# Decode attention products in four column groups: one step of a hybrid decoder trunk on one Trainium2 core

## The reference

```python
# differential attention, decode: 4 heads, two maps of 32 each, 1024 cached keys in pages of 128
past_k = cache_diff_k[page_table, l]; k_all = concat([past_k, ck]); v_all = concat([past_v, cv])
s = einsum('bqhmd,bkhmd->bhmqk', q, k_all) * 32 ** -0.5 + bias
p = softmax(s); o_c = einsum('bhqk,bkhe->bqhe', p[:, :, 0] - lam * p[:, :, 1], v_all)
# dilated window attention, decode: 4 heads of 64, the same form over the window buffer
# cross attention, decode: 4 heads of 256, 256 memory tokens
s = einsum('bthd,bmhd->bhtm', x @ w_q, mk) * 256 ** -0.5
o = einsum('bhtm,bmhd->bthd', softmax(s), mv)
```

## Time and profile before

| | |
|---|---|
| median of 3 runs | 2268.25 us (2266.75 to 2268.41) |
| span of the profiled execution | 2266.7 us |
| PE busy | 2038.1 us (90%), 11798 matmul records |
| PE weight load busy | 1717.2 us (76%) |
| DVE, ACT busy | 947.7 us (42%), 665.0 us (29%) |
| records of L728, L737, L752 (scores) | 192, 192, 256 |
| records of L807, L827 (values) | 512, 128 |

### The profile page before, as it was taken

One profiled execution on the slowest core, in us unless ns is written; L12 is line 12 of the kernel. 1 busy time (PEld: TensorE's weight loads), 2 busy tenths in 40 slices (PEclk: granted clock), 3 DMA queues, 4 the chain that ended last, 5 costly groups with the idle time before them and its releaser, 6 DMA issues.

```text
span 2266.7 us, 30760 instructions
## 1 busy us (share of the span) xinstructions
PE 2038.1 (90%) x11798; PEld 1717.2 (76%) x11798; DVE 947.7 (42%) x1514; ACT 665.0 (29%) x905; POOL 114.3 (5%) x220
## 2 busy tenths in 40 slices
PE   4999999788898988999979999988978989889998
PEld 3999977343686657999969998853447875679997
DVE  3554354212454235554355545332134542355544
ACT  2332242111233213332243323321122331133323
POOL 0000100000000000000100000000000000000000
PEclk8999999899698998999979999989977989889998
DMA  4443453555133532443424446345631435224432
GB/s 163 149 150 127 161 192 127 160 195 189 64 102 122 189 146 75 148 148 127 159 88 148 143 135 205 130 151 158 219 130 59 149 112 222 94 93 148 142 130 86
DMA packets 84412, 319.29 MB, mean 141 GB/s; under 512 B 10107, under 2 KB 45147, under 8 KB 59211
## 3 DMA queue, kind: packets, MB, share of 16 engines
q0 software_dynamic: 31104, 205.53, 26.6%
q1 hardware_dynamic: 53194, 112.24, 14.3%
HBM read 306.95 MB, written 10.79 MB: 140 GB/s over the span
## 4 chain that ended last, share of the span: by engine, by line
PE 86%; DVE 6%; issue 3%; ACT 3%; DMA 2%; SPq 0%; DVEq 0%; ACTq 0%
PE ps L556 18%; PE ps L558 18%; PE ps L557 18%; PE ps L807 6%; PE ps L525 5%; PE ps L728 3%; PE ps L650 3%; PE ps L652 3%; PE ps L651 3%; PE ps L752 2%; PE ps L827 2%; PE ps L737 2%; PE ps L835 1%; DVE bn L1286 1%; DMA hid<-bias_rows 1%
## 5 line engine op out<-in xcount | busy, mean ns | idle before, releaser
L556 PE MATMUL ps<-x_high,w_high 128*128 128x320 f32 x1408 | 439.5, 312 | 23.7 <-DVE w_low L1244 16.3
L557 PE MATMUL ps<-x_low,w_high 128*128 128x320 f32 x1408 | 438.6, 312 | 0.0
L558 PE MATMUL ps<-x_high,w_low 128*128 128x320 f32 x1408 | 438.5, 311 | 0.0
L995 ACT ACTIVATE w_high<-ring 128x2048 fp32r<-128x2048 f32 (+1 forms) x152 | 256.7, 1691 | 491.3 <-PE ps L558 478.7
L1244 DVE TENSOR_TENSOR w_low<-ring,w_high 128x2048 fp32r<-128x2048 f32 (+1 forms) x152 | 305.5, 2011 | 158.7 <-ACT w_high L995 158.3
L556 PEld LDWEIGHTS ps<-x_high,w_high 128*128 128x128 f32 x1408 | 267.7, 190 | 24.3 <-issue 24.3
L557 PEld LDWEIGHTS ps<-x_low,w_high 128*128 128x128 f32 x1408 | 267.7, 190 | 0.0
L558 PEld LDWEIGHTS ps<-x_high,w_low 128*128 128x128 f32 x1408 | 267.4, 190 | 0.0
L556 PE MATMUL ps<-h_high,w_high 128*128 128x320 f32 x704 | 220.0, 312 | 6.2 <-DVE h_low L1272 6.2
L503 POOL DMA_DIRECT2D ring<-in_w x216 | 114.1, 528 | 2114.3 <-PE ps L558 1913.6
L1251 DVE TENSOR_TENSOR m_low<-ring,m_high 128x1024 fp32r<-128x1024 f32 x112 | 137.0, 1224 | 193.4 <-ACT m_high L1038 193.4
(11 more groups left out here) (260 smaller groups left out, 2799.7 us busy)
## 6 DMA issues: line engine op xcount, KB each, us to landing
ring<-in_w POOLq DMA_DIRECT2D x152, 1024.0 KB, 5.1
ring<-in_w POOLq DMA_DIRECT2D x64, 704.0 KB, 4.3
cache<-in_dk SPq DMA_DIRECT2D x128, 128.0 KB, 2.2
cache<-in_dv SPq DMA_DIRECT2D x128, 128.0 KB, 2.4
cache<-in_ck SPq DMA_DIRECT2D x16, 1024.0 KB, 5.8
cache<-in_cv SPq DMA_DIRECT2D x16, 1024.0 KB, 6.9
cache<-in_wk SPq DMA_DIRECT2D x16, 768.0 KB, 6.2
cache<-in_wv SPq DMA_DIRECT2D x16, 768.0 KB, 5.0
```

The lines of the kernel that those rows point to most:

```text
L556: mm(out, wh, xh, start=first, stop=False)
L557: mm(out, wh, xl, start=False, stop=False)
L558: return mm(out, wl, xh, start=False, stop=last)
L995: fn(w_high[:, pos % 2, 0:n], ring[:, pos % RING, 0:n], ACT.Copy).then_inc(hi_w.sem, 1)
```

## The change

Each product of a decode item is divided by sample (b2) and head pair (hp) into four, of 32 rows each, on partitions 64 * b2 + 32 * hp onwards (`quarter`, `QUARTERS`), and the four are issued in turn, the loop over blocks outside.

- Scores: diff_dec takes the 32 columns of `qd` that belong to the pair; win_dec and cross_dec take their whole 32 columns, which leaves zero rows for the heads of the other pair (the score matrix has 128 rows now). Pairs no longer accumulate with each other. A sample's cache is waited for at its first product.
- Values: each quarter takes the 128 value columns of its own pair (512 in cross_dec, from 1024) and writes to its partitions; diff_dec and win_dec need one pair's columns only, and cross_dec one bank in place of two.
- win_dec's probabilities have 128 rows and are transposed in two batches, cross_dec's in one of two 128 x 128.
- DVE's `outputs` of diff_dec and win_dec spread the 128 columns back over 256 with the masks. cross_dec's masking product becomes a copy, `own_heads` on PE four transposes in place of eight products, and its `outputs` two times four small operations that pick the own rows.
- Tables (bias, masks, selectors) of win_dec grow to 128 rows. SP's loads, their order and their waits stay.

```diff
-BATCHES = [3 if k == "diff_dec" else 1 for k, _ in ITEMS]
+BATCHES = [{"diff_dec": 3, "win_dec": 2}.get(k, 1) for k, _ in ITEMS]
...
+                QUARTERS = [(b2, hp) for b2 in range(2) for hp in range(2)]
+                def quarter(b2, hp):
+                    return slice(64 * b2 + 32 * hp, 64 * b2 + 32 * hp + 32)
...
                     if kind == "diff_dec":
-                        for b2 in range(2):
-                            cache_in(k_ready, n, b2)
-                            r = 64 * b2
-                            for c in range(3):
-                                for hp in range(2):
...
-                                    last = mm(ps[r:r + 64, b0 + c, 0:(512 if c < 2 else NS)], qd[:, hp, 2 * n + b2, :], rhs,
-                                              start=(hp == 0), stop=(hp == 1))
+                        for c in range(3):
+                            for b2, hp in QUARTERS:
+                                if c == 0 and hp == 0:
+                                    cache_in(k_ready, n, b2)
+                                r = quarter(b2, hp)
...
+                                last = mm(ps[r, b0 + c, 0:(512 if c < 2 else NS)],
+                                          qd[:, hp, 2 * n + b2, 32 * hp:32 * hp + 32], rhs, start=True, stop=True)
...
                     elif kind == "cross_dec":
...
+                        for c4 in range(4):
+                            for b2, hp in QUARTERS:
...
+                                c = 4 * hp + c4
+                                last = mm(ps[quarter(b2, hp), b0, 0:256], qc[:, c, 2 * n + b2, :],
+                                          cache[:, b2, 256 * c:256 * c + 256], start=(c4 == 0), stop=(c4 == 3))
...
                         elif kind == "win_dec":
-                            for c in range(6):
-                                tr(ps[:, 6, 64 * c:64 * c + 64], p[0:64, P * c:P * c + P])
-                            last = tr(ps[0:NS, 6, 384:448], p[0:64, WK:WK + NS])
+                            for c in range(4 * b, min(4 * b + 4, 6)):
+                                last = tr(ps[:, 6, P * (c % 4):P * (c % 4) + P], p[:, P * c:P * c + P])
+                            if b:
+                                last = tr(ps[0:NS, 6, 256:384], p[:, WK:WK + NS])
...
                     if kind in ("diff_dec", "win_dec"):
-                        nk, w, v0 = (8, 64, 256) if kind == "diff_dec" else (6, 32, 0)
-                        for b2 in range(2):
-                            cache_in(v_ready, n if kind == "diff_dec" else 4 + n, b2)
-                            for k in range(nk + 1):
...
-                                last = mm(ps[w * b2:w * b2 + w, 7, 0:256], lhs, rhs, start=(k == 0), stop=(k == nk))
+                        nk, v0 = (8, 256) if kind == "diff_dec" else (6, 0)
+                        for k in range(nk + 1):
+                            for b2, hp in QUARTERS:
+                                if k == 0 and hp == 0:
+                                    cache_in(v_ready, n if kind == "diff_dec" else 4 + n, b2)
+                                r = quarter(b2, hp)
+                                at = P * k + r.start
...
+                                    lhs, rhs = t[:, at:at + 32], cache[:, 2 + b2, 256 * k + P * hp:256 * k + P * hp + P]
+                                last = mm(ps[r, 7, 0:P], lhs, rhs, start=(k == 0), stop=(k == nk))
...
                     elif kind == "cross_dec":
...
+                        for kb in range(2):
+                            for b2, hp in QUARTERS:
...
+                                last = mm(ps[r, bank, :], t[:, P * kb + r.start:P * kb + r.stop],
+                                          cache[:, 2 + b2, 1024 * kb + 512 * hp:1024 * kb + 512 * hp + 512],
+                                          start=(kb == 0), stop=(kb == 1))
...
-                    for c in range(KD):
-                        last = mm(ps[:, 7, 16 * c:16 * c + 16], own_x[i % 2][:, P * c:P * c + P], token_w[:, 0, 0:16],
-                                  start=True, stop=True)
+                    for c in range(4):
+                        last = tr(ps[:, 7, P * c:P * c + P], own_x[i % 2][:, P * c:P * c + P])
...
-                    for c in range(2):
-                        last = V.tensor_tensor(own_x[i % 2][:, 512 * c:512 * c + 512], ps[0:64, 1 + 3 * (i % 2) + c, :],
-                                               view(heads_w[:, 128 * c:128 * c + 1], [[64, 2], [0, 256]]), ALU.mult)
-                    last.then_inc(xv_done.sem, 1)
+                    V.tensor_copy(own_x[i % 2], ps[:, 1 + 3 * (i % 2), :]).then_inc(xv_done.sem, 1)
```

More of the change, by code:

```diff
@@ L203, in build @@
         pT = [arena[:, 2176:3328], arena[:, 3328:4480]]
-        own_x = [t[0:64, 128:1152] for t in pT]
+        own_x = [t[:, 256:768] for t in pT]
         kd = arena[:, 0:512].rearrange("p (g h d) -> p g h d", g=2, h=HX)
@@ L218, in build @@
         own_d = [hflat[:, 6144 + 256 * n:6400 + 256 * n] for n in range(3)] + [gate[:, 0, 0:256]]
-        own_w = [tflat[0:64, 2304 + 256 * n:2560 + 256 * n] for n in range(3)] + [gate[0:64, 1, 0:256]]
+        own_w = [tflat[:, 2304 + 256 * n:2560 + 256 * n] for n in range(3)] + [gate[:, 1, 0:256]]
         qxT = fm[:, :, 0:256]
@@ L747, in scores @@
                     elif kind == "cross_dec":
-                        for b2 in range(2):
-                            cache_in(k_ready, 8 + n, b2)
-                            r = 32 * b2
-                            for c in range(KD):
-                                last = mm(ps[r:r + 32, b0, 0:256], qc[:, c, 2 * n + b2, :],
-                                          cache[:, b2, 256 * c:256 * c + 256], start=(c == 0), stop=(c == KD - 1))
+                        for c4 in range(4):
+                            for b2, hp in QUARTERS:
+                                if c4 == 0 and hp == 0:
+                                    cache_in(k_ready, 8 + n, b2)
+                                c = 4 * hp + c4
+                                last = mm(ps[quarter(b2, hp), b0, 0:256], qc[:, c, 2 * n + b2, :],
+                                          cache[:, b2, 256 * c:256 * c + 256], start=(c4 == 0), stop=(c4 == 3))
                     else:
@@ L1423, in normalise @@
                     dve.wait_ge(e_done.sem, e_done.upto(l, i + 1))
-                    r1, k = {"diff_dec": (P, 1), "win_dec": (64, 1), "win_pro": (P, 2), "diff_pro": (P, 4),
-                             "cross_dec": (64, 1), "cross_pro": (P, 2)}[kind]
+                    r1, k = {"diff_dec": (P, 1), "win_dec": (P, 1), "win_pro": (P, 2), "diff_pro": (P, 4),
+                             "cross_dec": (P, 1), "cross_pro": (P, 2)}[kind]
                     link(V.reciprocal(st[0:r1, 12:12 + k], st[0:r1, 8:8 + k]))
```

139 lines of the change are left out of this document (73 added, 66 removed).

## The result

The median of the change is 2169.53 us (2163.16 to 2171.93) against 2268.33 beside it, a ratio of 0.956 (95% interval 0.955 to 0.958): 98.8 us saved, where I forecast 121 (2150, range 2110 to 2210). The profiled execution spans 2161.5 us, 105.2 less than the one of before, and is the quickest of the four; the steps are compared in it.

The account below looks back on a forecast made before the run. PE was taken to set the pace, transfers next. Savings of 11, 17, 17 and 15.5 us by stretch make 60.5 a layer, 121 for two, off the 2268.25 median: 2147, rounded 2150 us, range 2110 to 2210.

Parts of the forecast that it names:

- What bounds it next: Decode stages: after the change, SP's issue and cache transfers are late; waits for dk, dv, wv, ck, cv become PE's largest.
- Four abreast: Decode products: four column groups run side by side; a diff score takes about 2.1 us for 7.2.
- rival (1): Decode products: only two groups run at a time, as PE looks too few products ahead; 2190 us, chance 0.20.
- rival (2): Decode products: alternating groups are served one at a time, each paying an exposed weight load; 2310 us, chance 0.06.
- Values at 57 ns a record: Diff and window values: priced at the quickest record seen, 4.1 us for 8.41 (diff), 3.2 for 6.58 (window).
- First stretch: First decode stretch of a layer, 38.2 us: d0's scores and values shrink at 1.2 GHz; 11 saved, near 27.
- Second: Stretch d1 to d3, 71.2 us: page issue and landing set the period; 17 saved, near 54.
- Third: Window items and a diff_pro, 59.6 us plus 16.2 tail: periods of 10.2 waiting for wv; 17 saved, near 59 with tail.
- Cross: Cross items, 86.5 us: transfers hold three items, last cv in near 801; 15.5 saved, near 71.
- the clock term: Cross: six bursts behind a wait run at 1.2 GHz, up to 1.9 us each; half of that, 5.5 us, set aside.
- rival (3): Last three stretches: page calls get 20% longer under denser demand; 2175 us, chance 0.70 together with the forecast and rival (4).
- Rival (4): Every burst and cross's tail at 1.2 GHz: some 10 us a layer less gain, 2170; chance 0.70 with forecast and rival (3).

Follow-up runs that it names:

- e11: The change, loading only a quarter of the cached data of most decode items (output differs), beside the kernel before: 2051.2 us, ratio 0.905.
- e12: The kernel before, loading only the same quarter of the cached data: 2243.3 us, ratio 0.989.
- e5: The change plus overwritten identity products on PE ahead of waits for keys and values, to keep its clock up: 2160.8 us (the change 2169.5).
- e8: The change with the two 1 MB stores (out_mk, out_mv) issued only after the last cross values product: 2164.1 us (the change 2169.5).

## Why the prediction was right, and where it was off

*What bounds it next.* Right. DMA waits took the place of PE, in the five loads named (dk, dv, wv, ck, cv) and in wk, which I hadn't named. e11 and e12 show it without the trace: the gain is halved by the loads.

*Four abreast.* Right, against rival (1) (two at a time, 2190) and rival (2) (one at a time, 2310). The diff score of d0 takes 2.04 us, 2.1 forecast. The evidence I gave for rival (1) was misread, though: I took the hand-over of the earlier trace rows for a look-ahead of four or five records in all. With that the last group would start a round late, and it starts 0.02 us after the first, ahead of the second record of the first product. The rule of the Trainium skill in "TensorE: Matmul & The Clock Gate", "The mechanism" (matmuls in strict order, weight loads ahead of a running matmul only at other row groups), I took to mean one line for these products; four within 0.02 us at 394.17, all on the same rows, don't agree with that. Nor does the same page of the Trainium skill, whose section "Measured speedup vs the span model" has 2.38 for three column tiles: that is no single line. My estimate of 3 from it was below what was measured here, 7.2 us to 2.04, 3.5 times for four.

*Values at 57 ns a record.* The size was right by luck, the reason wrong. I took the upper end as a possible floor of issue; it is one group's stream at 1.2 GHz (53 ns with 0.21 a round), and at 2.4 GHz it is 27. The 4.1 I put for diff came out as 3.99 and 3.61, because PE had idled. For window items my 3.2 was too high where PE was warm: 1.87 in w0 and w1.

*First stretch.* 27 forecast, 25.5 measured in this profile, 28.3 to 28.7 in those of e5 to e8. I had d0's scores at 1.2 GHz and 3.8 us; here they ran at 2.4 (granted clock 1.00) in 2.04. Its values took 4.22, 4.1 forecast.

*Second.* 54 forecast, 56.2 measured. The keys were in 11.1 us after the scores (421.6 to 432.7), 11.0 forecast. What I mis-sized stands in the chain of the change:

```profile
430.48 2.21 DMA cache<-in_dk
...
453.35 4.29 DMA cache<-in_dv
```

The last page of dv takes 4.29 us to land where the last of dk takes 2.21: SP issues the next wk pair (1.5 MB) 0.6 us behind it. That is the 2 us, as read from the issue times. No run tried it alone, but two bear it out: the same page, with the pair 0.6 us behind it, in the kernel before (issued at 474.84) and in e11 (444.05), where the pair is a quarter and the item has four pages.

```profile
cache<-in_dv SPq DMA_DIRECT2D x1, 128.0 KB, 3.7
...
cache<-in_dv SPq DMA_DIRECT2D x1, 128.0 KB, 2.3
```

So most of it could have been read in the trace of before.

*Third.* 59 with its tail forecast, 59.9 measured. Three items take 10.2 to 10.7 us, 10.2 forecast. The path was another, so the size owes something to luck: I had each period wait for wv, with the next scores inside that wait. The chain of the first layer waits for two pairs of keys and one of values, the second layer's for one and two:

```profile
470.36 8.63 DMA cache<-in_wk
...
481.46 9.14 DMA cache<-in_wk
...
497.48 6.47 DMA cache<-in_wv
```

*Cross.* The step that was mis-sized: 15.5 us a layer forecast, 9.8 and 11.2 measured (86.5 to 76.7, 86.9 to 75.7). I followed the loads one by one and let each have the 6.9 us that a pair takes undisturbed; so the last cv was to be in 41.7 us after the start (801 against 759.3). The chain of the change:

```profile
716.34 1.97 PE ps L740 x32
...
718.99 8.86 DMA cache<-in_ck
727.89 3.45 PE ps L740 x28
...
732.14 7.05 DMA cache<-in_ck
739.23 1.95 PE ps L740 x28
...
742.01 9.15 DMA cache<-in_ck
751.21 3.43 PE ps L740 x28
...
755.60 2.73 PE ps L818 x16
...
759.02 8.70 DMA cache<-in_cv
767.76 3.63 PE ps L818 x12
```

It was in at 767.7, 51.4 after the start. Three loads took 8.86, 9.15 and 8.70 where 6.9 was reckoned, 6 us together. ck1 meets a weight load of 1 MB that POOL issued 2.1 us earlier; before, that load lay 6.4 us earlier, because d0's scores took that long, and ck1 took 6.88. ck3 goes out 2.1 us before cv1 is in. In the second layer it goes out 0.9 before, and takes no longer than an undisturbed one:

```profile
1804.18 6.78 DMA cache<-in_ck
```

cv3 meets the two stores, shown by e8, and had met them in the kernel before; there my 6.9 was a misreading, and no effect of the change. The other two collisions were read from the issue times, not tried. 3.0 us more are the bursts of 3.45 and 3.43 against 1.95 at 2.4 GHz, and 1.7 the one of 3.63 (granted clock 0.50 to 0.55 over each): together 4.7 of the 5.5 that I had set aside for the clock. The burst of 2.73 is not the clock's (granted 1.00 over it); sample 1's values, 9.37 us on their way, are in only 0.75 us after its start. So the clock term was nearly right, and the term mis-sized was the transfers': for ck1 and ck3 the denser schedule brought loads together that had lain apart, for cv3 I had missed a collision that was there. This was rival (3), 2175, in its mechanism, though not where I put it: the pages of a call came at 0.47 to 0.57 us as before, and the large transfers paid.

*The sum.* Of the 121 the profiled run shows 105.2. Cross falls 10.0 short over both layers (5.7 and 4.3), the mixers 2.6 (1.4 and 1.2); the last 3 lie outside these stages. The median lies 6 above the profiled run. That would be its short first stretch if the other three executions had the long one, which isn't shown, as they have no trace; their granted clock over the run is 0.891 to 0.895, its own 0.901.

*The clock.* Rival (4) put 10 us a layer on it, and that its 2170 is the time measured is luck: in cross the clock took no more than was set aside, and the loads took the rest. e5 gives back 9 over both layers, with some 8 lost again to its own products; what the clock alone is worth stays open.

## What to carry to other kernels

Before dividing products to run abreast, ask which operand arrives last: work that can run while the rest of the data comes in needs no more speed, and here two streams of an early half were worth as much as four of the whole. When the engine that set the pace becomes quick, cost the transfers as one schedule, with every other load and store that falls beside them, and not each at its undisturbed time; two of the collisions here could be read in the trace of before. To see what is left behind them, load a quarter in both kernels: it prices the transfers (25 us before, 118 after) where the sum of waits (45 us a layer of the 59) understates them.

## What was new of the hardware

Four fp32 streams of 32 columns each start within 0.02 us and keep full pace, 27 ns a record of 128 columns over all groups at 2.4 GHz. Issued group by group, scores ran two abreast (4.68 us for 24 records), and values one at a time, with 0.33 us from the start of the last product over 64 rows to the next group's first. And a page that lands 2.2 us after its issue alone needed 4.3 with a 1.5 MB pair issued 0.6 us behind it, as a load of 1 MB that lands in 6.8 to 7.0 needed 8.7 with two stores of 1 MB behind it (e8).
